# Two more blocks turned on VectorE and carried, one of them with its steps a chunk later, and the first chunks' rounding interleaved

## What is computed

```python
def hybrid_mixer(xn, w_in, ...):
    proj = xn @ w_in
    dn_qkv, dn_z, dn_a, dn_b, swa_q, swa_kv, sb_qkv, gates = split_cols(proj, IN_SIZES)
    dn_qkv = jax.nn.silu(causal_dwconv(dn_qkv, dn_conv))        # 4 taps along the positions
    q, k, v = split_cols(dn_qkv, ...)
    q, k = l2norm(q), l2norm(k)                                 # per head of 128
    g = -exp(dn_a_log) * softplus(dn_a + dn_dt_bias)
    o_dn = gated_delta_rule(q, k, v, g, sigmoid(dn_b))
    ...

def memory_cross_attention(hn, mem_n, w_xq, w_xkv, w_xo):
    q = (hn @ w_xq).reshape(bsz, seq, X_HEADS, X_DH)            # 4 heads of 128
    kv = (mem_n @ w_xkv).reshape(...)
    s = einsum('bqhd,bmhd->bhqm', q, kv[:, :, 0]) * X_DH ** -0.5
    p = softmax(s)
    return einsum('bhqm,bmhd->bqhd', p, kv[:, :, 1]) @ w_xo
```

## Time and profile before

| | us |
|---|---|
| median of 3 executions | 2494.46 (2493.82 to 2494.64) |
| the profiled execution | 2494.04 |
| its span | 2492.2 |
| PE busy | 2481.5 |
| PEld busy | 2051.3 |
| ACT busy | 1541.5 |
| DVE busy | 1490.1 |
| POOL busy | 33.4 |

### The profile page before, as it was taken

The page is one execution under the profiler, slowest core; times in us unless marked ns, Lnnn a source line. Parts: engine busy times, 40 slices in busy tenths (PEclk is TensorE's granted clock), DMA queues, the critical chain, the costliest instruction groups (busy, mean ns, idle before and its releaser), DMA issues.

```text
span 2492.2 us, 29745 instructions
## 1 busy us (share of the span) xinstructions
PE 2481.5 (100%) x12494; PEld 2051.3 (82%) x12494; DVE 1490.1 (60%) x1223; ACT 1541.5 (62%) x2041; POOL 33.4 (1%) x41
## 2 busy tenths in 40 slices
PE   9999999999999999999999999999999999999998
PEld 7887788888888888888888888888888888888887
DVE  5775656545545545666765665545565677646675
ACT  6645777636537547766465565535587688638873
POOL 0000000000000000000000000000000000000000
PEclk9999999999999999999999999999999999999999
DMA  8554555555555555545444445555655555555554
GB/s 287 187 200 163 187 200 187 199 188 196 192 193 196 190 199 187 201 169 187 154 160 145 155 162 193 193 196 189 267 188 185 186 188 199 187 198 191 195 193 152
DMA packets 69366, 472.37 MB, mean 190 GB/s; under 512 B 7912, under 2 KB 8352, under 8 KB 13424
## 3 DMA queue, kind: packets, MB, share of 16 engines
q1 hardware_dynamic: 67040, 460.62, 51.6%
q0 software_dynamic: 1312, 7.73, 0.8%
q10 hardware_dynamic: 880, 2.11, 0.2%
HBM read 468.33 MB, written 2.11 MB: 189 GB/s over the span
## 4 chain that ended last, share of the span: by engine, by line
PE 98%; DVE 1%; ACT 1%; issue 1%; DMA 0%; SPq 0%; POOLq 0%; POOL 0%; DVEq 0%; ACTq 0%
PE acc L528 31%; PE acc L530 31%; PE acc L529 31%; PE tp L812 1%; PE tp L548 0%; PE tp L745 0%; DMA x_raw<-in_x_turned 0%; PE tp L684 0%; PE tp L693 0%; DVE cv L1965 0%; DVE w_lo L1677 0%; PE tp L563 0%; PE tp L564 0%; PE tp L612 0%; PE tp L960 0%
## 5 line engine op out<-in xcount | busy, mean ns | idle before, releaser
L1677 DVE TENSOR_TENSOR w_lo<-w_raw,w_hi 128x2048 fp32r<-128x2048 f32 x430 | 983.6, 2289 | 730.9 <-ACT w_hi L1044 729.0
L1044 ACT ACTIVATE w_hi<-w_raw 128x2048 fp32r<-128x2048 f32 x430 | 823.0, 1916 | 482.4 <-DMA w_raw<-in_stream 462.3
L528 PE MATMUL acc<-w_hi,x_hi 128*128 128x512 f32 (+1 forms) x2240 | 875.1, 391 | 0.7 <-DVE w_lo L1684 0.4
L530 PE MATMUL acc<-w_hi,x_lo 128*128 128x512 f32 (+1 forms) x2240 | 868.4, 388 | 0.0
L529 PE MATMUL acc<-w_lo,x_hi 128*128 128x512 f32 (+1 forms) x2240 | 868.3, 388 | 0.0
L528 PEld LDWEIGHTS acc<-w_hi,x_hi 128*128 128x128 f32 x2240 | 420.6, 188 | 89.6 <-issue 2.0
L530 PEld LDWEIGHTS acc<-w_hi,x_lo 128*128 128x128 f32 x2240 | 420.6, 188 | 86.6
L529 PEld LDWEIGHTS acc<-w_lo,x_hi 128*128 128x128 f32 x2240 | 420.7, 188 | 85.5 <-issue 1.0
L528 PE MATMUL acc<-w_hi,a_hi 128*128 128x512 f32 x1120 | 436.3, 390 | 0.1
L530 PE MATMUL acc<-w_hi,a_lo 128*128 128x512 f32 x1120 | 435.7, 389 | 0.0
L529 PE MATMUL acc<-w_lo,a_hi 128*128 128x512 f32 x1120 | 435.7, 389 | 0.0
(11 more groups left out here) (383 smaller groups left out, 1301.3 us busy)
## 6 DMA issues: line engine op xcount, KB each, us to landing
w_raw<-in_stream SPq DMA_DIRECT2D x430, 1024.0 KB, 4.8
w_raw<-in_stream SPq DMA_DIRECT2D x16, 256.0 KB, 8.1
h<-in_x SPq DMA_DIRECT2D x4, 512.0 KB, 14.0
frow<-in_rows POOLq DMA_DIRECT2D x2, 1024.0 KB, 6.2
m_raw<-in_mem_turned POOLq DMA_DIRECT2D x1, 2048.0 KB, 10.2
memt<-in_mem POOLq DMA_DIRECT2D x1, 2048.0 KB, 8.9
x_raw<-in_x_turned SPq DMA_DIRECT2D x3, 512.0 KB, 8.3
dec<-gc_rows ACTq DMA_DIRECT2D x1, 1024.0 KB, 6.1
```

What stands on the lines that cost most here:

```text
L528: pe.matmul(dst, xh, wh[:, k], start=first and k == 0, stop=False)
L530: mm = pe.matmul(dst, xl, wh[:, k], start=False, stop=last and k == n_k - 1)
L1044: act.activation(w_hi[:, c % SLOTS], w_raw[:, c % SLOTS], ACT.Copy).then_inc(hi_ready, 1)
L1677: dve.tensor_tensor(w_lo[:, c % SLOTS], w_raw[:, c % SLOTS], w_hi[:, c % SLOTS].bitcast(F32), ALU.subtract).then_inc(lo_ready, 1)
```

## The change

- Queries of the cross attention: no `xqT` group on PE. At c = 8 DVE turns the block and carries two quadrants, ACT carries the other two, both with the scale 128 ** -0.5; `half_carried` uses `tensor_scalar` in place of `tensor_copy` for all its callers.
- Delta rule, block 0 only: no `("dT", 0)`. DVE turns the block at c = 4, ACT carries it in two lots at c = 4 and c = 5; the first tap and the others come at c = 5, tanh and SiLU at c = 6, the transposes back and the squares at c = 7, their sum at c = 8. The taps read `dmoved` in SBUF.
- The beginning: for all four early chunks a tile of x and a quarter of the weights alternate; 13 opening matmuls in place of 16.

```diff
@@ PE
-            for _ in range(16):
+            for _ in range(13):
                 pe.matmul(acc[:, 1, 0, :], junk[:, 0:P], junk[:], start=True, stop=True)
@@ PE, dn_side
-                for b in range(6):
+                for b in range(1, 6):
                     if c == 4 * b + 4:
                         accs.wait(pe, accs.name[("dn", b)])
                         transposes(tps.name[("dT", b)], nat[:, b % 2])
                 for b in range(4):
-                    if c == 4 * b + 6:
+                    if c == (4 * b + 6 if b else 7):
                         pe.wait_ge(conv_out, b + 1)
@@ PE, cross attention
                 if c == 9:
-                    tps.wait(pe, tps.name["xqT"])
+                    pe.wait_ge(b_half, LAST["xq"])
+                    pe.wait_ge(b_moved, SIDE["xq"] + 1)
...
-                if c == 8:
-                    accs.wait(pe, accs.name["xq"])
-                    transposes(tps.name["xqT"], nat[:, 1])
@@ ACT, beginning (DVE alike)
-            def turned_high(c):
+            for c in range(EARLY):
                 for k in range(4):
                     t = 4 * c + k
...
                     act.activation(x_hi[:, t], x_raw[:, t], ACT.Copy, scale=col[:, t:t + 1]).then_inc(x0_high, 1)
-                    if c == 0:
-                        split_part(0, k)
-
-            turned_high(0)
-            for c in range(1, EARLY):
-                turned_high(c)
-                for k in range(4):
                     split_part(c, k)
@@ ACT, dn_side
+                if c in (4, 5):
+                    carried("dn0", dmoved[:], dturned[:], (0, 1) if c == 4 else (2, 3))
                 for b in range(6):
...
-                    if c == 4 * b + 4:
+                    if c == (4 * b + 4 if b else 5):
...
+                        src = tp[:, tps.name[("dT", b)] % 2] if b else dmoved
                         for k in range(4):
                             w = COL["dn_conv"] + 4 * (4 * b + k) + 3
-                            ins = act.activation(cv[:, k], tp[:, g % 2, k], ACT.Copy, scale=col[:, w:w + 1])
+                            ins = act.activation(cv[:, k], src[:, k], ACT.Copy, scale=col[:, w:w + 1])
                         ins.then_inc(conv0, 1)
-                    if c == 4 * b + 5:
-                        tps.wait(act, g)
+                    if c == (4 * b + 5 if b else 6):
+                        if b:
+                            tps.wait(act, tps.name[("dT", b)])
+                        else:
+                            act.wait_ge(dn_taps, 1)
...
                         act.activation(th[:], cv[:], ACT.Tanh, scale=0.5).then_inc(conv_t, 1)
@@ ACT, cross attention
+                if c == 8:
+                    carried("xq", xqT[:], xkturned[:], (0, 1), scale=128 ** -0.5)
@@ DVE, dn_side, behind the steps of c == 4 and c == 5 on u and g
+                if c == 4:
+                    accs.wait(dve, accs.name[("dn", 0)])
+                    dve.transpose(dturned[:].rearrange("p (m n) -> p m n", m=M), nat[:, 0]).then_inc(b_turned, 1)
@@ DVE, cross attention
                 if c == 8:
-                    g = tps.name["xqT"]
-                    dve.wait_ge(tp_done, g + 1)
-                    dve.tensor_scalar(flat(xqT[:]), tpf(g), 128 ** -0.5, None, ALU.mult).then_inc(tps.sem(g), 1)
+                    accs.wait(dve, accs.name["xq"])
+                    dve.wait_ge(b_moved, SIDE["xk"] + 1)
+                    dve.transpose(xkturned[:].rearrange("p (m n) -> p m n", m=M), nat[:, 1]).then_inc(b_turned, 1)
+                    half_carried("xq", xqT[:], xkturned[:], scale=128 ** -0.5)
```

More of the change, by code:

```diff
@@ L171, in build @@
         zz = sb("zz", [P, M, 1024], F32, a_a + 8 * K)
+        dturned = sb("dturned", [P, M * N], F32, a_a + 16 * K)
+        dmoved = sb("dmoved", [P, 4, SEQ], F32, a_a + 20 * K)
         state = sb("state", [P, 8, P], F32, a_a + 24 * K)
@@ L226, in build @@
         took = {k: {e: [sem(f"{k}_took_{e}{p}") for p in range(2)] for e in ("act", "dve")} for k in ("acc", "tp")}
-        cols_in, cst_in, mask_in, gla_in, row_in, out_done = [sem(s) for s in ("cols_in", "cst_in", "mask_in", "gla_in", "row_in", "out_done")]
+        cols_in, cst_in, mask_in, gla_in, row_in, out_done, dn_taps = [sem(s) for s in ("cols_in", "cst_in", "mask_in", "gla_in", "row_in", "out_done", "dn_taps")]
         x_in = sem("x_in")
@@ L317, in build @@
         SIDE = {name: k for k, name in enumerate([("y", n) for n in range(4)] + [("norm1", n) for n in range(4)] + [("norm3", n) for n in range(3)]
-                                                 + ["sbq", "sbk"] + [("ydn", n) for n in range(2)] + [("merged", n) for n in range(4)] + [("norm5", n) for n in range(4)] + ["xk"] + [("norm6", 3)])}
-        ROUNDED = {name: k for k, name in enumerate(name for name in SIDE if name not in ("sbq", "sbk", "xk"))}
-        LAST = {("norm1", 3): 1, ("merged", 3): 2, ("norm6", 3): 3}
+                                                 + ["dn0"] + ["sbq", "sbk"] + [("ydn", n) for n in range(2)] + [("merged", n) for n in range(4)] + [("norm5", n) for n in range(4)] + ["xk", "xq"] + [("norm6", 3)])}
+        ROUNDED = {name: k for k, name in enumerate(name for name in SIDE if name not in ("dn0", "sbq", "sbk", "xk", "xq"))}
+        LAST = {("norm1", 3): 1, ("merged", 3): 2, "xq": 3, ("norm6", 3): 4}
         def ready(c, k=3):
@@ L358, in build @@
         add("ab_rows", "ab", who="act")
-        add(("dT", 0))
         add(("nN", 0), who="act")
@@ L389, in build @@
         add("wo_")
-        add("xqT")
         add(("xs", 0), ("xs", 1), who="act")
@@ L1073, in high, with carried @@
                         ins.then_inc(xh_done, 1)
-            def carried(name, dst, src, quadrants):
+            def carried(name, dst, src, quadrants, scale=1.0):
                 if 0 in quadrants:
@@ L1082, in carried @@
                     for to in range(4):
-                        ins = act.activation(dst[32 * to:32 * to + 32, :, :, q], src[32 * q:32 * q + 32, :, :, to], ACT.Copy)
+                        ins = act.activation(dst[32 * to:32 * to + 32, :, :, q], src[32 * q:32 * q + 32, :, :, to], ACT.Copy, scale=scale)
                 if 3 in quadrants or name in LAST:
@@ L1340, in dn_side @@
                     ins.then_inc(xT_spread, 1)
+                if c in (4, 5):
+                    carried("dn0", dmoved[:], dturned[:], (0, 1) if c == 4 else (2, 3))
                 for b in range(6):
-                    g = tps.name[("dT", b)]
                     if c == 4 * b + 3:
-                        if b >= 2:
+                        if b == 2:
+                            act.wait_ge(b_turned, SIDE["dn0"] + 1)
+                        elif b > 2:
                             act.wait_ge(tp_done, tps.name[("dT", b - 2)] + 1)
@@ L1365, in dn_side @@
                         act.activation(th[:], cv[:], ACT.Tanh, scale=0.5).then_inc(conv_t, 1)
-                    if c == 4 * b + 6 and b < 4:
+                    if b < 4 and c == (4 * b + 6 if b else 7):
                         g = tps.name[("nN", b)]
@@ L1720, in norm_turned, with half_carried @@
                 dve.transpose(turned[n % 2][:].rearrange("p (m n) -> p m n", m=M), h[:, :, n * N:(n + 1) * N]).then_inc(b_turned, 1)
-            def half_carried(name, dst, src):
+            def half_carried(name, dst, src, scale=1.0):
                 dve.wait_ge(b_turned, SIDE[name] + 1)
@@ L1728, in half_carried @@
                     for to in range(4):
-                        ins = dve.tensor_copy(dst[32 * to:32 * to + 32, :, :, q], src[32 * q:32 * q + 32, :, :, to])
+                        ins = dve.tensor_scalar(dst[32 * to:32 * to + 32, :, :, q], src[32 * q:32 * q + 32, :, :, to], scale, None, ALU.mult)
                 ins.then_inc(b_half, 1)
@@ L1808, in _ @@
             dve.wait_ge(gain_in, 16)
-            def turned_low(c):
-                for t in range(4 * c, 4 * c + 4):
+            for c in range(EARLY):
+                for k in range(4):
+                    t = 4 * c + k
                     dve.wait_ge(x0_high, t + 1)
                     dve.scalar_tensor_tensor(x_lo[:, t], x_raw[:, t], col[:, t:t + 1], x_hi[:, t].bitcast(F32), ALU.mult, ALU.subtract).then_inc(x0_low, 1)
[L1813 to L1819, removed]
                     split_part(c, k)
@@ L1964, in dn_side @@
                                 w = COL["dn_conv"] + 4 * (4 * b + k) + 3 - sh
-                                ins = dve.scalar_tensor_tensor(cv[:, k, sh:], tp[:, g % 2, k, 0:SEQ - sh], col[:, w:w + 1],
+                                ins = dve.scalar_tensor_tensor(cv[:, k, sh:], src[:, k, 0:SEQ - sh], col[:, w:w + 1],
                                                                cv[:, k, sh:], ALU.mult, ALU.add)
@@ L1968, in dn_side @@
                                 link(ins)
-                        ins.then_inc(tps.sem(g), 1)
-                    if c == 4 * b + 5:
+                        ins.then_inc(tps.sem(tps.name[("dT", b)]) if b else dn_taps, 1)
```

(3 more changed lines are left out.)

6 lines of the change are left out of this document (3 added, 3 removed).

## The result

Each kernel was timed in six executions on one chip. The kernel before took 2494.60 us in the median (2493.82 to 2496.05), the changed one 2505.57 us (2504.38 to 2506.78). The ratio is 1.0044, with an interval of 1.0033 to 1.0054: slower by 11.0 us. The forecast was 2502.5 with a range up to 2504.5. The direction holds, the size doesn't: 3.1 us more were lost than forecast, and the time lies 1.1 us outside the range.

What follows compares the result with a forecast made beforehand. PE's chain of waits, 98% of it on PE, was taken as the bound. Chain 7.3, queries -0.45 and beginning -0.1 made 6.75 us, with 1.5 for the clock 8.3: 2502.7, or 2502.5 if only some executions pay; range 2499.0 to 2504.5.

Steps and rivals of the forecast that it cites:

- Step 1: PE's transposes before chunk 5 and of the cross attention's queries: both on the path, removing each saves 0.85 us.
- Step 2: Delta rule, block 0: DVE's transpose and ACT's copies delay chunk 7 and the transposes back; chunk 8 starts 7.3 us later.
- Step 3: Cross attention's queries: PE 0.85 us earlier, then 0.4 us of wait at xp's second transposes; net -0.45 us, bounds -0.85 and +0.1.
- Step 4: Kernel's beginning: interleaved rounding and fewer warm-up matmuls gain little, the first weight piece's landing sets chunk 1; -0.1 us.
- Step 5: PE's wait before the delta rule's transposes back: if the clock falls in it, 1.5 us more, bounds 0 and 2.5.
- more lost: Rival: clock low longer than at the start, or falling also near chunk 7, and queries' copies dear; 2505.5 us, chance 0.06.

Runs made afterwards that it cites:

- the block alone: The kernel before with only block 0 of the delta rule turned on DVE and carried, its steps one chunk later: 2505.11 us, ratio 1.0043.
- the first lot alone: The changed kernel plus 8 spare PE products in the wait before chunk 7 only: 2504.58 us, -0.43 us to the changed kernel.
- both lots: The changed kernel plus spare PE products in both new waits, 8 before chunk 7 and 22 before the transposes back: 2501.49 us, -3.52 us to the changed kernel.
- the second lot alone: The changed kernel plus 16 spare PE products only in the wait before the transposes back: 2501.31 us, -3.70 us to the changed kernel.

## Why the prediction was too low

**Step 1, the transposes removed: right.** Chunk 5 gains 0.85 us beyond what the beginning gives (-1.47 for the -0.62 at `ab`), the queries 0.80 us; 0.85 was said for each.

**Step 2, the chain: right in each of its steps.** Time lines of ACT and DVE in the changed kernel, answering to the earlier trace rows:

```profile
1109.01 0.44 ACT L1059 ACTIVATE ab<-tp,rstd 128x16 f32<-128x16 f32 x2 [4.28 <-PE tp L574]
1110.84 3.41 ACT L1081 ACTIVATE dmoved<-dturned 32x256 f32<-32x256 f32 x8 [1.40 <-DVE dturned L1953]
...
1117.79 1.90 ACT L1042 ACTIVATE w_hi<-w_raw 128x2048 fp32r<-128x2048 f32 x1
1119.72 3.39 ACT L1081 ACTIVATE dmoved<-dturned 32x256 f32<-32x256 f32 x8
1123.14 1.71 ACT L1355 ACTIVATE cv<-dmoved,col 128x256 f32<-128x256 f32 x4
```

```profile
1109.57 1.24 DVE L1953 STREAM_TRANSPOSE dturned<-nat 128x1024 f32<-128x1024 f32 x1
...
1124.96 5.07 DVE L1962 SCALAR_TENSOR_TENSOR cv<-dmoved,col,cv 128x255 f32<-128x255 f32 x12 [2.35 <-ACT cv L1355]
1129.95 2.28 DVE L1677 TENSOR_TENSOR w_lo<-w_raw,w_hi 128x2048 fp32r<-128x2048 f32 x1
1132.15 1.22 DVE L1971 SCALAR_TENSOR_TENSOR cqT<-th,cv 128x1024 f32<-128x1024 f32 x1
```

All of it stands 0.62 us earlier than walked, which is the beginning's gain in this execution. Shifted by that, the walk gives 1109.6 for the transpose, 1110.9 for the copies, 1122.1 for chunk 7 and 1133.3 for `("nN", 0)`; the rows say 1109.57, 1110.84, 1122.08 and 1133.42. The transpose sits idle behind `u` as said. The waits were 2.2, 5.6 and 0.9 us by the walk and are 2.0, 5.6 and, at full clock, 0.54. The first tap took 1.71 us for the 1.57 walked, the dear end of the bounds given. With the clock kept up the block alone costs 7.7 us, for 7.3, and the whole change 7.1 us (2501.49 for 2494.39), for 6.75.

**Step 3, the queries: right in mechanism, a little over half in size.** The wait on `xp` came where it was said, 0.46 us for 0.4, and costs 0.55: net -0.26 us for -0.45, within the bounds.

DVE's scaled copies cost what plain ones do, at the cheap end of the two that were given:

```profile
1921.65 1.24 DVE L2286 STREAM_TRANSPOSE xkturned<-nat 128x1024 f32<-128x1024 f32 x1
1922.92 2.38 DVE L1729 TENSOR_SCALAR xqT<-xkturned 32x256 f32<-32x256 f32 x8
```

**Step 4, the beginning: mis-sized, the other way.** I took -0.1 us and -0.5 as the bound; it is -0.66 in the medians of the part alone. This helped by luck: it hid 0.6 us of what step 5 missed. I argued that the first weight piece lands at 11.7 and so sets chunk 1. That was the landing of one execution. In six traces with the old order chunk 1 starts 3.0 us after ACT's first rounding of chunk 1's x, in each one (10.18 and 13.19 before; 10.84 and 13.86 with the delta rule alone), since four roundings of x stand ahead of the first piece:

```profile
10.84 1.71 ACT L1161 ACTIVATE x_hi<-x_raw,col 128x256 fp32r<-128x256 f32 x4 [0.38 <-DMA x_raw<-in_x_turned]
```

In the new order it is 2.3 us when the weights are there, and 1.4 us behind the first piece when they are late. The changed kernel's profile shows the first case:

```profile
10.41 0.51 ACT L1158 ACTIVATE x_hi<-x_raw,col 128x256 fp32r<-128x256 f32 x1 [0.39 <-DMA x_raw<-in_x_turned]
11.10 0.63 ACT L1047 ACTIVATE w_hi<-w_raw 128x512 fp32r<-128x512 f32 x1 [0.17 <-DMA w_raw<-in_stream]
```

There chunk 1 starts at 12.74. Its starts with the new order are 12.74, 12.95, 13.74, 13.30, 12.90, 13.00 and 13.07 in seven traces, 13.1 on average; with the old one 13.19, 13.55, 13.86, 14.09, 13.91 and 14.17 in six, 13.8. The difference of 0.7 us agrees with the medians. Counted from ACT's first rounding of chunk 1's x it is 3.0 us in the old order and 2.5 on average in the new, so 0.55 us of it is the order's, and the rest is x that happened to land earlier in these traces.

**Step 5, the clock behind the new wait: this is the step that failed.** I said: if it falls I take 1.5 us, bounds 0 and 2.5. It costs 3.5 us by the medians (2505.01 and 2501.49), 2.8 for the block alone (+10.5 and +7.7) and 2.8 in the traces up to the end of chunk 8. Two things were wrong in it. I took the length of the low level from the kernel's start, 5.1 us, and it was 6.9 and 10.2 us; after a fall inside the wait 7.3 us of it still lay on work, not 4.0. The pace was right: 0.45 x 7.3 = 3.3 us, less the 0.54 us of waiting for the square that the slower transposes swallow, gives the 2.8 of the traces. And I gave the fall a chance of little more than one in two (0.50 and 0.06), where it was there in all four traces with this wait and no spare products in it (both of the changed kernel, the block alone, the first lot alone). The other executions of these kernels point the same way: all 20 that the medians take in have a mean granted clock of 0.996 or 0.997, against 0.999 with both lots. The rival that was right is the last, more lost (2505.5), to which I had given 0.06: its first condition, a clock low for longer, came true; its second, a fall near chunk 7, came true in three of the four traces with the wait there unfilled (the first of the changed kernel, the block alone, the second lot alone) and costs nothing; its third, the queries at their dear end, didn't.

Put together, against the 8.3 us of the sum: the chain +0.4, the queries +0.2, the beginning -0.55 and the clock +2.0 give 10.4 of the 11.0 us measured.

The silence of 3.4 us before the fall at the end was no bound either: 2.0 us were enough in three traces, and did nothing in a fourth. That the moment shifts agrees with the Trainium skill ("TensorE: Matmul & The Clock Gate", Part 1, What's actually happening), by which the windows run freely; I had cited it and drawn from it only that some executions would not pay. Here all paid, and what shifted was the moment. The same section has an idle array throttled; here the falls in chunk 7 came when PE had been at work again for 0.5 to 1.2 us, so the measurement goes further than what it says.

Left open: the medians say 3.5 us and the two profiled executions differ by 2.4 us at their end (2504.38 and 2502.02), one of them 0.6 us under its median and the other 0.5 us over. The slowest execution on that chip, 2506.07 us, has a mean granted clock of 0.996 for the 0.997 of the other three, which hints at a longer low level; no trace shows it. The 0.96 us pause at L745 in the first profile, with nothing that ends it but "issue", isn't in the second; what it is isn't known.

## What to carry to other kernels

When a kernel has one engine at 98% of its chain, a new wait on that engine is to be priced twice: its length, and the time for which the engine's clock is low behind it, which here added 3.5 us to waits of 2.0 and 5.6. Before moving work to another engine, look for where that engine is idle *in its program order*: the transpose and sixteen copies cost some 9 us, the clock's share with them, behind `u` and all on ACT, and next to nothing a few instructions earlier and shared with DVE. A landing time taken from one trace is a sample, so a bound that rests on its falling within 0.1 us of another event is no bound.

## What was not expected of the hardware

- The clock fell 3.0 us after the start of a silence of 2.0 us, 1.0 us after PE had resumed (1123.0), and in another execution of the same kernel, with the same silence, not at all. With the block alone it fell 0.5 us after PE had resumed (1123.8 for 1123.30), with the second lot alone 1.2 us (1124.0 for 1122.75).
- Once low, it stayed low for 3.4, 6.9 and 10.2 us, with PE at work for most or all of that time.
- Spare f32 products of 128x128, 0.23 us each, kept it at 1.00 through waits of 2.0 and 5.6 us (8 and 22 of them). With 16 in the second wait alone six executions of seven took 2500.58 to 2502.41 us at a mean granted clock of 0.998 to 0.999, and one 2504.98 at 0.997, the reading of the kernels in which the second fall is there; so 16 seem not to have been enough every time.
- In the first microseconds the first weight piece of chunk 1 was taken up by ACT 0.69 us after x tile 4 in one trace of the changed kernel (10.41 and 11.10) and 1.42 us after it in the other (10.47 and 11.89).
